# A product-key expert layer: v rows gathered expert-major and summed by 32-column matmuls

## The chip, the cores and the metric

The kernel runs on one core of a Trainium2 chip. The metric is the device time of one launch in microseconds, median of three runs.

## The reference, cut to what matters

One step of a transformer trunk over 512 prompt frames and 64 sample frames, width 1024, float32. Per layer: an input projection, two kinds of attention (8 heads of width 64, 4 heads of width 128), an output projection, LayerNorm, and then a PEER layer (product-key retrieval of single-neuron experts) and a second LayerNorm. The PEER layer is where the change lies. Each frame picks 16 experts in each of 8 heads, so 128 of 16,384; every expert is one row of `u_tab` and one of `v_tab`, 1024 floats (4 KB) each:

```python
q = (xs @ w_pq).reshape(PEER_BLOCK, PEER_HEADS, 2, PEER_QDIM // 2)
sc = jnp.einsum('thpd,hpnd->thpn', q, sub_keys)      # scores of 2 x 128 keys a head
s, i = lax.top_k(sc, PEER_TOPK)
...                                                   # top 16 of the 16 x 16 sums: eidx, g
hid = jnp.einsum('td,thkd->thk', xs, u_tab[eidx])
a = (g * gelu(hid)).astype(xs.dtype)
return jnp.einsum('thk,thkd->td', a, v_tab[eidx])
```

## The kernel before, in words

The frames are worked in five blocks: 0 to 3 are 128 prompt frames each, block 4 (`SMP`) is the 64 sample frames, laid twice on the 128 partitions. A block's PEER work is 128 *slots*; in slot k every partition (frame) deals with its own k-th expert. Block 4 has 64 slots, each half of the partitions taking half of a frame's experts. That makes 576 slots (`JSLOTS`).

A slot costs one gather of 128 u rows and one of 128 v rows (POOL, `gather`, L1670; an indirect DMA of 128 x 4 KB, its row numbers one column of `idx`). VectorE multiplies the u rows with x1 and sums along the row (L1598), which gives one column of `hid`. ScalarE applies Gelu to four columns at once (L1200) and multiplies each by the gate weight g, giving `coef` (L1208). Then the v rows are weighted and added in one of two ways, chosen by `on_tensor(k)`: on PE for 464 of the 576 slots, with a 128x128 diagonal of the coefficients that ScalarE makes (L1229) as stationary operand and two 512-column halves into the accumulator `acc` (L959, `j_tensor`); the profile shows two passes per float32 matmul, so four records a slot. On VectorE for the other 112, which multiplies by `coef` and adds into `y_acc` (L1610). `y_acc` starts as ALPHA * x1 on ScalarE (L1221); `f_vector` adds `acc` to it and takes the statistics; `n_vector` and `n_tensor` apply the LayerNorm; `y_store` writes it out.

All engines' instruction lists are written by one planner, `weave`: each lane (x projection, a attention, o output, w query, t top-k, j slots, f and n final norm) has a start and an end on a common axis of slot steps (`spans`), and each engine issues the lanes' steps in the order of their marks. An engine works in order, so one waiting instruction holds all behind it. In lane j, VectorE takes u row k at step k+3 and v row k is used at step k+11 (`V_LAG`). POOL issues u row j and then v row j-8 (`V_AT`), one after the other. Block p+1's attention and projections run among block p's slots.

Buffers: six u rows (`URING`) and six v rows (`VRING`) of 4 KB per partition, to which spare tiles are added late (`U_MORE`, `V_MORE`). A gather waits until the row before it in its buffer has been used. Weights stream on SP's queue through `wring`, five tiles of 512 KB; four of the eight w_v tiles (`HELD`) stay resident in `held`. Block 1's first 14 projection tiles are loaded early into buffers that lie idle then.

## Time and profile before

| | |
|---|---|
| runs | 1899.32 us median (1895.7 to 1900.65, three runs) |
| profiled execution, first to last instruction | 1895.5 us; its time with what lies around it isn't shown apart, the runs' median is 3.8 us above |
| mean granted PE clock | 0.964 |
| PE busy | 1601.3 us (84%), 6192 matmuls |
| VectorE (DVE) busy | 1263.2 us (67%) |
| ScalarE (ACT) busy | 627.4 us (33%) |
| GpSimd (POOL) busy | 1245.3 us (66%) |
| DMA | 744.60 MB, mean 393 GB/s; indirect gathers 605.75 MB |

Busy shares are means over unlike stages. A matmul's end is modelled, and consecutive ones overlap, so PE's busy time is not PE at its peak. A releaser behind an arrow is what ended an engine's idle time. In the windows the engines stand in the order PE, PE weight load, DVE, ACT, POOL, and of a filtered window only the engine asked for stands there.

### The profile page before, as it was taken

To read this page: it belongs to the slowest core of one execution; us is meant where nothing else is said; L and a number is where in the kernel's file an instruction comes from. 1 tells how busy PE (TensorE), PEld (TensorE's weight loads), DVE (VectorE), ACT (ScalarE), POOL (GpSimd) and SP (SyncE) were. 2 spreads that over 40 slices of the span, in tenths; PEclk is the share of its full clock that TensorE was granted. 3 is DMA by queue.
4 is the path that set the end of the run, shared out by engine and by line. 5 is a ranking of instruction groups with operands and counts; after the bars stand their busy time and mean duration, and the time that the engine had idled before them with its cause. 6 is when DMAs were issued, how large, how long until landed. Compare 5 with 4: busy or idle time off the path is not lost.

```text
span 1895.5 us, 20537 instructions
## 1 busy us (share of the span) xinstructions
PE 1601.3 (84%) x6192; PEld 881.4 (47%) x6192; DVE 1263.2 (67%) x2836; ACT 627.4 (33%) x1771; POOL 1245.3 (66%) x1199
## 2 busy tenths in 40 slices
PE   8999779879978698888898889998689877767877
PEld 7596445536435355355354465634436422222322
DVE  2379984576767755868587647589756897655543
ACT  1432561223237422232276222136522232222211
POOL 3027676576677755777777665677777777777771
PEclk9999999999989999999999998998899999999999
DMA  9899999999999999999999999999999999999995
GB/s 318 309 347 371 410 393 387 410 409 409 386 412 409 409 401 409 406 408 409 411 406 393 397 406 377 406 409 370 405 411 409 409 410 409 409 409 409 410 409 225
DMA packets 210197, 744.60 MB, mean 393 GB/s; under 512 B 24640, under 2 KB 29544, under 8 KB 209960
## 3 DMA queue, kind: packets, MB, share of 16 engines
q0 software_dynamic: 166720, 605.75, 80.9%
q1 hardware_dynamic: 43368, 137.53, 19.0%
q8 instruction: 51, 0.84, 0.2%
q14 instruction: 58, 0.48, 0.1%
HBM read 736.03 MB, written 7.75 MB: 392 GB/s over the span
## 4 chain that ended last, share of the span: by engine, by line
DMA 35%; PE 30%; POOL 20%; issue 9%; DVE 6%; ACT 1%; SPq 0%; DVEq 0%; ACTq 0%
DMA vbuf<-in_peer_v,idx 18%; PE acc L959 10%; POOL ubuf L1670 9%; POOL vbuf L1670 8%; DMA ubuf<-in_peer_u,idx 8%; PE mixer L667 5%; DMA held<-in_peer_u,idx 4%; PE mixer L833 2%; PE mixer L936 2%; DVE ubuf L1598 2%; PE mixer L683 2%; DMA wring<-in_c_k 1%; POOL wring L1670 1%; DMA held<-in_peer_v,idx 1%; POOL held L1670 1%
## 5 line engine op out<-in xcount | busy, mean ns | idle before, releaser
L959 PE MATMUL acc<-vbuf,diag 128*128 128x512 f32 x1308 | 644.5, 627 | 159.5 <-DMA vbuf<-in_peer_v,idx 154.6
L1670 POOL DMA_INDIRECT ubuf<-in_peer_u,idx x518 | 553.9, 1069 | 255.5 <-issue 138.4
L1670 POOL DMA_INDIRECT vbuf<-in_peer_v,idx x478 | 512.4, 1072 | 264.4 <-PE acc L959 133.0
L1598 DVE CUSTOM_DVE_ANT_0 ubuf<-ubuf,x 128x1024 f32<-128x1024 f32 x332 | 404.9, 1224 | 252.9 <-DMA ubuf<-in_peer_u,idx 249.7
L959 PEld LDWEIGHTS acc<-vbuf,diag 128*128 128x128 f32 x1308 | 236.7, 196 | 470.4 <-issue 429.0
L1598 DVE CUSTOM_DVE_ANT_0 ubuf<-ubuf,mixer 128x1024 f32<-128x1024 f32 x186 | 225.6, 1218 | 118.2 <-DMA ubuf<-in_peer_u,idx 81.9
L1200 ACT ACTIVATE act_h<-hid 128x4 f32<-128x4 f32 x144 | 29.5, 205 | 504.1 <-DVE hid L1598 503.4
L936 PEld LDWEIGHTS mixer<-stage,wring 128*128 128x128 f32 x1280 | 149.5, 193 | 17.4 <-issue 15.4
L936 PE MATMUL mixer<-stage,wring 128*128 128x128 f32 x1280 | 150.6, 276 | 0.7 <-DMA wring<-in_w_pq 0.6
L1229 ACT ACTIVATE diag<-ident,coef 128x128 f32<-128x128 f32 x392 | 138.4, 395 | 22.1 <-PE acc L959 18.1
L1610 DVE SCALAR_TENSOR_TENSOR y_acc<-vbuf,coef,y_acc 128x1024 f32<-128x1024 f32 x99 | 127.3, 1286 | 18.1 <-DMA vbuf<-in_peer_v,idx 16.0
L667 PEld LDWEIGHTS mixer<-xT,wring 128*128 128x128 f32 x1056 | 123.4, 194 | 18.0 <-issue 18.0
L667 PE MATMUL mixer<-xT,wring 128*128 128x128 f32 (+1 forms) x1056 | 124.5, 277 | 5.7 <-DMA wring<-in_w_qk 5.7
L1208 ACT ACTIVATE coef<-act_h,g 128x1 f32<-128x1 f32 x576 | 122.8, 283 | 16.2
L1670 POOL DMA_INDIRECT held<-in_peer_v,idx x60 | 64.3, 1072 | 18.3 <-issue 15.9
L1164 ACT COPY stage<-mixer 128x256 f32<-128x256 f32 x40 | 14.9, 373 | 181.9 <-PE mixer L936 181.9
L959 PE MATMUL acc<-held,diag 128*128 128x512 f32 x92 | 47.7, 649 | 24.5 <-DMA held<-in_peer_v,idx 22.7
L1200 ACT ACT_TABLE_LOAD x52 | 66.7, 1283 | 0.9
L833 PE MATMUL mixer<-wring,stage 128*128 128x512 f32 x128 | 58.5, 602 | 1.7 <-DMA wring<-in_w_out 1.5
L1598 DVE CUSTOM_DVE_ANT_0 wring<-wring,mixer 128x1024 f32<-128x1024 f32 x30 | 36.6, 1222 | 30.8 <-DMA wring<-in_peer_u,idx 21.6
L720 PE MATMUL mixer<-kv,q_pad 128*128 128x128 f32 (+3 forms) x128 | 48.8, 464 | 6.3 <-DVE neg_max L1337 5.7
L959 PE MATMUL acc<-vbuf,xT 128*128 128x512 f32 x80 | 40.5, 631 | 14.1 <-DMA vbuf<-in_peer_v,idx 14.0
(266 smaller groups left out, 1959.1 us busy)
## 6 DMA issues: line engine op xcount, KB each, us to landing
wring<-in_w_pq SPq DMA_DIRECT2D x80, 512.0 KB, 8.1
wring<-in_w_qk SPq DMA_DIRECT2D x66, 512.0 KB, 7.6
wring<-in_w_out SPq DMA_DIRECT2D x40, 512.0 KB, 7.5
wring<-in_w_v SPq DMA_DIRECT2D x20, 512.0 KB, 7.5
ubuf<-in_peer_u,idx POOLq DMA_INDIRECT x518, 13.0
vbuf<-in_peer_v,idx POOLq DMA_INDIRECT x478, 12.7
wring<-in_c_k SPq DMA_DIRECT2D x8, 512.0 KB, 6.9
wring<-in_c_v SPq DMA_DIRECT2D x8, 512.0 KB, 7.9
```

Of the source, the lines that this page charges most:

```text
L667: last = pe.matmul(ps_o[:, q % 2, j * P:j * P + frames], w[:, c, :], xT[:, c, 0:frames], start=c == 0, stop=c == KT - 1)
L683: last = pe.matmul(ps_o[0:frames, hf, :], xT[:, k, 0:frames], w[:, c, :], start=k == 0, stop=k == KT - 1)
L720: last = pe.matmul(dst, q_pad[:, g_, half, :], kT[:, g_, 0:nk], start=True, stop=not fox)
L833: last = pe.matmul(sums[hf], mix[:, c, :], w[:, hf * 512:(hf + 1) * 512], start=c == 0, stop=c == KT - 1)
L936: last = pe.matmul(ps_o[:, t % 2, j * P:(j + 1) * P], w[:, c, :], mixT[:, c, :], start=c == 0, stop=c == KT - 1)
L959: last = pe.matmul(sums[hf], diags[D_PLAN[n][0]], v_buf[b][:, hf * 512:(hf + 1) * 512], start=first, stop=last_one)
L1200: nc.scalar.activation(act_h[:, c:c + GRP], hid[:, c:c + GRP], ACT.Gelu).then_inc(gelu_done, 1)
L1208: last = nc.scalar.activation(coef[:, c + i:c + i + 1], act_h[:, c + i:c + i + 1], ACT.Copy, scale=g[p % 2][:, at + i:at + i + 1])
L1229: nc.scalar.activation(diags[b], (ident2 if p == SMP else ident)[:, :], ACT.Copy, scale=coef[:, v % MARKS:v % MARKS + 1]).then_inc(diag_do ...
L1598: nc.vector.tensor_tensor_reduce(out=u, in0=u, in1=x, scale=1.0, scalar=0.0, op0=ALU.mult, op1=ALU.add, accum_out=hid[:, k % MARKS:k % MAR ...
L1610: nc.vector.scalar_tensor_tensor(y_acc[p % 2][:, :], v_buf[b], coef[:, v % MARKS:v % MARKS + 1], y_acc[p % 2][:, :], ALU.mult, ALU.add).th ...
L1670: pool.indirect_dma_start(buf, None, a[table], bass.IndirectOffsetOnAxis(ap=idx[p % 2][:, at:at + 1], axis=0)).then_inc(landed_, 16)
```

## The change

The v rows change sides. A *unit* is 32 slots. The unit's row numbers are transposed in 32x32 blocks on VectorE (`idx_v`), so one gather now brings, on the 32 partitions of each quarter, the 32 experts of one frame: four frames of 32 experts each instead of 128 frames of one (block 4: as many, with two frames of twice 32). The coefficients are transposed the same way and spread by VectorE into `mix_w`, a 128x32 stationary operand per row whose four (two) non-zero columns pick the frame. A v row is then summed by matmuls with 32 output columns, that is into 32 partitions of `acc`; which 32 goes round with k (`group_of`). PE takes two rows at a time (`QUAD = 2`), the halves outermost, so consecutive matmuls go to different groups. All 576 v rows go this way, none is added on VectorE, and no diagonal is made.

The frames stand in another order in `acc`, so ALPHA * x1 is placed in it by a permuted diagonal (`place`) as the block's first matmul; ScalarE copies `acc` out into `x1[p % 3]`, which replaces `y_acc`; and y is stored in 16 pieces of 8 frames (block 4: 4 of 16). Gelu runs once per unit of 32 columns. Because a unit's coefficients are there only when its 32 u rows are done, v row k is gathered beside u row k+32 (`V_AT` = 32, `V_LAG` = 35). The v ring has eight buffers instead of six, the u ring loses one late buffer, and `HELD` goes from 4 to 3.

```diff
-HELD = 4
+HELD = 3
-URING, VRING = 6, 6
-U_MORE, V_MORE = ((368, 1), (438, 2)), ((360, 3), (430, 3))
+URING, VRING = 6, 8
+U_MORE, V_MORE = ((438, 2),), ((360, 3), (430, 3))
+UNIT, QUAD = 32, 2
-U_LAG, H_LAG = 3, 2
-D_LAG = U_LAG + H_LAG + GRP - 1
-V_LAG = D_LAG + 3
+U_LAG = 3
+G_LAG, C_LAG = U_LAG + 1, U_LAG + 2
+V_LAG = UNIT + U_LAG
 V_AT = V_LAG - U_LAG
...
+def frame_of(k):
+    s = k % UNIT
+    return s % 2 * 16 + s // 2 if part_of(k) == SMP else s % 4 * 8 + s // 4
+def group_of(k):
+    return k % UNIT % (2 if part_of(k) == SMP else 4)
...
 def y_store(sp, p):
+            for j in range(runs):
+                for q in range(many):
+                    ...
+                    sp.dma_start(o["y"][to:to + rows, :], y[at:at + rows, :]).then_inc(out_y[p % 2], 16)
...
 def j_tensor(pe, _):
             for j in range(J_STEPS):
-                v = j - V_LAG
-                if v >= 0 and on_tensor(v):
+                v = j - V_LAG - QUAD + 1
+                if v >= 0 and v % QUAD == 0:
+                    if v == p * SLOTS:
+                        ...
+                        wait(pe, acc_read, 2 * p)
+                        for hf in range(2):
+                            ...
+                                pe.matmul(acc[:, c], place[:, :], x1[p % 3][:, c], start=True, stop=False)
+                    pe.wait_ge(w_made, v // 8 + 1)
+                    for k in range(v, v + QUAD):
+                        b, _, nth = V_PLAN[k]
+                        pe.wait_ge(v_in[b], 16 * (nth + 1))
                     for hf in range(2):
-                        last = pe.matmul(sums[hf], diags[D_PLAN[n][0]],
-                                         v_buf[b][:, hf * 512:(hf + 1) * 512], start=first, stop=last_one)
-                    last.then_inc(vP_used, 1)
+                        for k in range(v, v + QUAD):
+                            s, r = k % UNIT, 32 * group_of(k)
+                            last = pe.matmul(acc[r:r + 32, hf * 512:(hf + 1) * 512], mix_w[:, s * 32:(s + 1) * 32],
+                                             v_buf[V_PLAN[k][0]][:, hf * 512:(hf + 1) * 512], start=False,
+                                             stop=k >= end - (2 if p == SMP else 4))
+                            if hf:
+                                last.then_inc(vP_used, 1)
...
 def j_scalar(act, _):
+                k = j - G_LAG
+                if 0 <= k < JSLOTS and k % UNIT == UNIT - 1:
+                    act.wait_ge(u_used, k + 1)
+                    wait(act, coef_done, n - 1)
+                    nc.scalar.activation(act_h[:, h], hid[:, h], ACT.Gelu).then_inc(gelu_done, 1)
...
 def f_scalar(act, p):
+            act.wait_ge(vP_used, min((p + 1) * SLOTS, JSLOTS))
+            for hf in range(2):
+                nc.scalar.copy(y[0:frames, c], acc[0:frames, c]).then_inc(acc_read, 1)
...
 def decode(n, s):
+                    for w in pairs_ready(p, n):
+                        c = slice(w * UNIT, (w + 1) * UNIT)
+                        nc.vector.transpose(idx_v[p % 2][:, c], idx[p % 2][:, c]).then_inc(idxv_done, 1)
...
 def j_vector(dve, chain):
-                    nc.vector.scalar_tensor_tensor(y_acc[p % 2][:, :], v_buf[b], coef[:, v % MARKS:v % MARKS + 1],
-                                                   y_acc[p % 2][:, :], ALU.mult, ALU.add).then_inc(vD_used, 1)
+                k = j - C_LAG
+                if 0 <= k < JSLOTS and k % UNIT == UNIT - 1:
+                    dve.wait_ge(gelu_done, n + 1)
+                    link(nc.vector.tensor_tensor(coef[:, :], act_h[:, h], g[p % 2][:, at:at + UNIT], ALU.mult))
+                    nc.vector.transpose(coef_t[:, :], coef[:, :]).then_inc(coef_done, 1)
+                    dve.wait_ge(coef_done, n + 1)
+                if k >= UNIT - 1 and (k + 1) % 8 == 0:
+                    wait(dve, vP_used, (n - 1) * UNIT + 8 * (c + 1))
+                    ...
+                    nc.vector.tensor_tensor(diagonals(p, c), each, to, ALU.mult).then_inc(w_made, 1)
...
 def gather(pool, table, k):
+                if k % UNIT == 0:
+                    pool.wait_ge(idxv_done, k // UNIT + 1)
+                at += frame_of(k) - k % UNIT
+                rows = idx_v[p % 2][:, at:at + 1]
```

## Rows read from the trace of the kernel before

**Rows 1.** the page's 40 slices: DMA busy in tenths, and GB/s moved

```profile
DMA  9899999999999999999999999999999999999995
GB/s 318 309 347 371 410 393 387 410 409 409 386 412 409 409 401 409 406 408 409 411 406 393 397 406 377 406 409 370 405 411 409 409 410 409 409 409 409 410 409 225
```

**Rows 2.** windows: range, us, busy us (count) by engine, clock, DMA share, GB/s

```profile
0.00:110.00 110.00, 102.17 (x617) 76.56 (x618) 33.47 (x130) 30.01 (x90) 17.54 (x47) 1.00 0.91 313
110.00:205.00 95.00, 87.98 (x524) 65.64 (x523) 88.73 (x281) 30.64 (x78) 61.80 (x57) 0.98 0.98 374
205.00:350.00 145.00, 123.09 (x541) 75.47 (x541) 99.94 (x200) 64.70 (x179) 96.19 (x91) 0.99 1.01 397
350.00:1500.00 1150.00, 992.93 (x3924) 558.91 (x3923) 798.47 (x1740) 407.29 (x1092) 801.72 (x724) 0.96 1.02 403
1500.00:1870.00 370.00, 276.52 (x553) 97.14 (x552) 236.20 (x479) 91.53 (x326) 268.02 (x282) 0.97 1.03 410
```

**Rows 3.** the chain of waits, share of the span by engine

```profile
DMA 35%; PE 30%; POOL 20%; issue 9%; DVE 6%; ACT 1%; SPq 0%; DVEq 0%; ACTq 0%
```

**Rows 4.** groups of instructions: count, busy us, mean ns, idle before

```profile
L959 PE MATMUL acc<-vbuf,diag 128*128 128x512 f32 x1308 | 644.5, 627 | 159.5 <-DMA vbuf<-in_peer_v,idx 154.6 <-ACT diag L1229 4.6
L1610 DVE SCALAR_TENSOR_TENSOR y_acc<-vbuf,coef,y_acc 128x1024 f32<-128x1024 f32 x99 | 127.3, 1286 | 18.1 <-DMA vbuf<-in_peer_v,idx 16.0
L1229 ACT ACTIVATE diag<-ident,coef 128x128 f32<-128x128 f32 x392 | 138.4, 395 | 22.1 <-PE acc L959 18.1
L1208 ACT ACTIVATE coef<-act_h,g 128x1 f32<-128x1 f32 x576 | 122.8, 283 | 16.2
```

**Rows 5.** timeline of PE, one v row: start us, us, count, idle before

```profile
787.15 1.96 PE L959 MATMUL acc<-vbuf,diag 128*128 128x512 f32 x4 [0.60 <-DMA vbuf<-in_peer_v,idx]
```

**Rows 6.** timeline of VectorE: a product of 128x32 elements

```profile
132.10 0.19 DVE L1550 TENSOR_TENSOR best_v<-best_v,sum 128x32 f32<-128x32 f32 x1
```

**Rows 7.** windows of POOL's gathers alone: u rows, then v rows twice

```profile
112.00:204.60 92.60, 32.13 (x32) 0.98 0.98 375
...
112.00:204.60 92.60, 29.34 (x24) 0.98 0.98 375
...
350.00:1500.00 1150.00, 398.68 (x362) 0.96 1.02 403
```

**Rows 8.** windows of VectorE's v additions (L1610) alone

```profile
110.00:205.00 95.00, 10.24 (x8) 0.98 0.98 374
```

**Rows 9.** DMA issues: count, KB each, median us to landing

```profile
wring<-in_w_v SPq DMA_DIRECT2D x20, 512.0 KB, 7.5
```

**Rows 10.** windows of pieces under full rate

```profile
500.00:520.00 20.00, 20.00 (x48) 8.93 (x47) 14.53 (x29) 4.97 (x18) 14.33 (x14) 1.00 0.96 354
1170.00:1190.00 20.00, 20.00 (x113) 14.26 (x112) 13.66 (x48) 5.94 (x14) 10.48 (x10) 1.00 0.93 338
1300.00:1320.00 20.00, 18.27 (x75) 11.63 (x74) 19.79 (x29) 11.38 (x25) 12.62 (x10) 0.85 0.92 319
```

**Rows 11.** the end: POOL, DMA landing, PE, VectorE and SP

```profile
1850.13 0.93 POOL L1670 DMA_INDIRECT held<-in_peer_v,idx  x1 [0.30 <-issue]
1861.33 0.94 POOL L1670 DMA_INDIRECT wring<-in_peer_v,idx  x1 [1.63 <-PE mixer L959]
...
wring<-in_peer_v,idx POOLq DMA_INDIRECT x1, 17.9
...
1869.34 5.39 PE L959 MATMUL mixer<-held,xT 128*128 128x512 f32 x12 [0.61 <-DMA held<-in_peer_v,idx]
1874.56 5.31 PE L959 MATMUL mixer<-vbuf,xT 128*128 128x512 f32 x12
...
1885.06 1.29 DVE L1623 TENSOR_TENSOR y_acc<-y_acc,mixer 128x512 f32<-128x512 f32 x2 [15.89 <-PE mixer L959]
...
1892.01 0.48 SPq L622 DMA_DIRECT2D out_y<-y_acc  x1
```

**Rows 12.** windows of PE's v rows (L959) alone

```profile
350.00:1500.00 1150.00, 551.14 (x1117) 203.44 (x1116) 0.96 1.02 403
```

More of the change, by code:

```diff
@@ L59, in parts_of, with pairs_ready @@
     return ((0, 1), (1, 3), (3, 8)) if p == 0 else ((0, 4), (4, 8)) if p == SMP else ((0, 8),)
+def pairs_ready(p, n):
+    if p == SMP:
+        return range(PAIRS // 2) if n else ()
+    h0, h1 = parts_of(p)[n]
+    return range(h0 // 2, h1 // 2)
 def t_plan(p):
@@ L223, in spans @@
         end = float(min((p + 1) * SLOTS, JSLOTS) + V_LAG)
[L224 to L226 removed]
+        out.append(("f", p, 3, end + 1.0, end + 4.0))
+        rows = 433.0 if p == SMP - 2 else end + 5.0 if p > SMP - 2 else (p + 1) * SLOTS + 78.0
         out.append(("n", p, 2, rows, rows + (3.0 if p in (1, SMP) else 10.0)))
@@ L291, in build @@
         x1 = [sb(f"x1_{n}", [P, D]) for n in range(3)]
-        y_acc = [sb(f"y_acc{n}", [P, D]) for n in range(2)]
         stage = sb("stage", [P, 5 * SEQ])
@@ L352, in build @@
         idx = [sb(f"idx{n}", [P, SLOTS], U32) for n in range(2)]
+        idx_v = [sb(f"idx_v{n}", [P, SLOTS], U32) for n in range(2)]
         g = [sb(f"g{n}", [P, SLOTS]) for n in range(2)]
@@ L1612, in j_vector @@
                 yield
         def f_vector(dve, p, chain):
-            link, y, n = chain.link, y_acc[p % 2], p % 2
-            end = min((p + 1) * SLOTS, JSLOTS)
-            dve.wait_ge(vP_used, PE_COUNT[end])
-            wait(dve, vD_used, end - PE_COUNT[end])
-            if p == SMP:
-                dve.wait_ge(acc_made, NB)
-            if p == SMP:
-                for hf in range(2):
-                    last = nc.vector.tensor_tensor(y[:, hf * 512:(hf + 1) * 512], y[:, hf * 512:(hf + 1) * 512], acc_s[hf], ALU.add)
-            else:
-                last = nc.vector.tensor_tensor(y[:, :], y[:, :], acc[:, :], ALU.add)
@@ L1626, in f_vector @@
-            last.then_inc(acc_read, 1)
-            dve.wait_ge(acc_read, p + 1)
+            link, y, n = chain.link, x1[p % 3], p % 2
+            yield
+            dve.wait_ge(acc_read, 2 * p + 2)
             for hf in range(2):
```

215 lines of the change are left out of this document (91 added, 124 removed).

## The prediction, made before the changed kernel ran

> **What bounds the kernel now.** I read the page first. The DMA line of its 40 slices is at 9 nearly throughout, and the line below it stands at about 409 GB/s from the fifth slice on [rows 1]. Then the windows by stage. From 1500 to 1870 us, where only table rows are gathered, 410 GB/s is held; no longer stretch is faster, so I take 410 GB/s as full rate. One gathered row tile (128 x 4 KB = 524,288 bytes) then costs 1.28 us of DMA, and a slot (one u, one v) 2.56 us. In the same windows PE is busy 75 to 93%, VectorE 64 to 93% [rows 2]. The chain of waits says the same less directly: DMA holds its largest share, PE the second [rows 3]. The groups and the timeline of PE show why PE is second: a v row costs it four passes, 1.96 us, and then it idles 0.60 us for the next one's DMA [rows 4, 5]. So PE follows DMA in the light stretches. The kernel is bound by bytes, except where the rate falls under 410. Valued as (1 - rate/410) x length [rows 2]: 26.0 us before 110 us (set-up, not touched), 8.3 us from 110 to 205, 4.6 us from 205 to 350, 19.6 us from 350 to 1500, none from 1500 to 1870. After that comes a drain. Work taken off an engine can therefore return at most what those losses and the drain hold, and whatever moves bytes out of a full stretch costs nothing, but out of a stretch into the end of the list costs its full price.
>
> **The change part by part.**
>
> *VectorE and ScalarE.* 112 of the 576 v rows are added on VectorE now, 144 us (110 of them show as two groups at 1.286 us, one of them [rows 4]). They go. In their place, per unit of 32 slots, stand six small operations (coefficient product, transpose, four weight fills of 128x32 elements). The trace has no such transpose; a 128x32 product took 0.19 us [rows 6], so about 1.2 us a unit, 22 us for 18 units; even at twice that VectorE gives back 100 us. ScalarE loses 464 diagonals at 0.395 us and 576 coefficients at 0.283 us [rows 4] (346 us) and gets 18 Gelus. Neither engine bounds in the mean, so this is worth only what it does inside the lossy stretches. Per unit VectorE now waits for one Gelu; behind it in its queue are the next u dot products, on which POOL's u gathers wait. The ring of six u buffers (6 x 1.28 us) covers a wait of a few us; I charge nothing, and without that cover it would be 18 waits.
>
> *PE.* 112 more rows go to PE, but each pair is written to two different 32-partition groups, the halves interleaved (row a, row b, row a, row b). If two column groups run beside each other, a pair costs about what a row costs now: one 1.96 us burst [rows 5]. 288 bursts instead of 464: PE gets lighter by some 340 us. Whether they do run beside each other no row of this trace shows: from below 1.96 us a pair, from above two serial rows, 3.9 us. I take the lower, because the operands, the number of passes and the bank are those of today's burst and only the output partitions differ; the upper is the first rival. The two extra start matmuls a block (place x x1) replace ScalarE's multiplication and go into the same accumulator: 5 x 1 us, hidden under PE's idle.
> The Trainium skill, "TensorE: Matmul & The Clock Gate", Part 3, speaks for and against: it reports three 32-column tiles at 2.38 times one, but also that a weight load overlaps matmuls in flight only when its row group differs, which column tiles of one contraction never do. By the first a pair is about 2 us, by the second it comes near the serial price. No row here decides.
>
> *The order of gathers.* Before, v row k is gathered beside u row k+8, now beside u row k+32. So in the first 32 steps u rows come alone and 32 v rows come alone at the end. Between 112 and 204.6 us, POOL issued 32 u rows and 24 v rows [rows 7]. Those 24 now come later: 24 x 1.28 = 30.7 us of DMA time put behind a bandwidth-bound remainder. What is won against it: in this stretch VectorE is busy 88.7 of 95 us (top-k of block 0, u dots), 10.2 of which are v additions [rows 2, 8]. VectorE, not DMA, then sets the pace, so step 32 is reached about 11 us earlier (between 10.2 and, if all idle time went too, 16.5). PE was full there as well, but it drops its v rows and is not late. Net +19.7 us (14 to 20.5).
>
> *Bytes.* HELD goes from 4 to 3, so one more w_v tile is streamed in blocks 1 to 4: 4 x 1.28 = +5.1 us. The w_v group shows today's four tiles in each of five blocks [rows 9]. The y stores carry the same bytes in 16 small DMAs a block; SP has idle time for them except at the end.
>
> *Losses that shrink.* 4.6 + 19.6 = 24.2 us are lost between 205 and 1500 us. The worst pieces: 338 GB/s at 1170 us with PE full, 354 at 500 us with PE full and VectorE decoding, 319 at 1300 us with VectorE at 19.8 of 20 us [rows 10]. PE at half the price per row and eight v buffers instead of six cure the first kind; the top-k and memset bursts of VectorE remain, the u ring stays at six, and one late u buffer is dropped. I take half: -12 us (0 to -24).
>
> *The end.* Now: the last v gather is issued at 1861.33 and lands 17.9 us later, at 1879.2; PE, which has been nine rows behind since 1869.34, is waited for until 1885.06; the end is 1895.5 [rows 11]. After: PE is level with DMA, because the coefficients of the last 32 slots are ready long before their rows. POOL issues a gather in 0.93 + 0.30 = 1.23 us [rows 11], still under 1.28, so v rows alone keep the full rate. Behind the last landing: one burst 1.96, then the same 10.5 us of norm and store, with the 1.29 us addition replaced by two ScalarE copies of about the same length, and three more store issues of 0.48 us [rows 11]: 1.96 + 10.5 + 1.4 = 13.9 against 16.3 us today: -2.4 us (-0.5 with the upper price of a pair).
>
> *Sum* on the profiled execution's span: 1895.5 + 19.7 + 5.1 - 12 - 2.4 = 1905.9 us. The median of the runs is 3.8 us above that span (1899.32); the same offset gives 1909.7 us, +0.5%. The likeliest case's own range is 1899 to 1921.
>
> **Rivals.**
>
> *1. The pairs do not overlap on PE.* Then every row costs at least the back-to-back price, (1874.56 - 1869.34)/3 = 1.74 us [rows 11], and there are 112 more of them. From 350 to 1500 us PE does 1117/4 = 279 of 362 v rows [rows 7, 12] and idles 1150 - 993 = 157 us; 83 more rows want 144 us of it. For: PE is already full in the pieces of rows 10. Against: much of its idle time is spread evenly and can be used. If a quarter of it shows as delay, +36; nothing is recovered, +12; and 32 v rows alone at the end pace by PE, 32 x (1.74 - 1.28) = +15. 1909.7 + 63 = about 1973 us. It decides once a pair costs over 2.56 us in the v-only end; from 350 to 1500 us PE's other work takes 993 - 551 = 442 us [rows 2, 12], so 181 pairs fill the rest at (1150 - 442)/181 = 3.9 us each, and bite earlier where that work is dense. (By the skill's rule on weight loads, told above, it would come out this way.)
>
> *2. The losses go entirely and the start costs less.* Step 32 at 16.5 us less, all 24.2 us recovered: 1895.5 + 14.2 + 5.1 - 24.2 - 2.4 + 3.8 = 1892 us, 0.4% faster. For: VectorE loses a tenth of its work in every lossy piece. Against: the 1300 us and 500 us pieces are VectorE's own bursts. It needs both, since either alone stays above 1893.6.
>
> *3. The unit's chain is exposed.* VectorE waits in order for ScalarE's Gelu, and PE for VectorE's weights. If 1.5 us a unit shows: 18 x 1.5 = 27, about 1937 us. For: ScalarE takes the Gelu behind its attention work in program order. Against: rings of six u and eight v rows hold some 18 us of DMA work.
>
> **How the numbers follow.** Forecast 0.52, rival 1 0.23, rival 2 0.20, rival 3 0.05. A difference under 0.3% (5.7 us: 1893.6 to 1905.0) can't be told from none. The lower part of the forecast's own range, about 0.2, and a little of rival 2 fall there: same 0.22. Faster, nearly all rival 2: 0.19. Slower: 0.59. The range must take in rival 2 in part and most of rival 1, which ends anywhere from 1950 up: 1889 to 1965.
>
> **What would show it.** Right: bytes up by 2.1 MB; from 112 us to the 32nd u gather about 81 us instead of 92.6, at under 310 GB/s; v groups on PE with bursts of eight passes (two rows) of about 2 us and PE busy some 300 us less; 410 GB/s until the last landing, with v rows alone for some 41 us, and about 14 us behind it. Wrong: bursts of eight passes that last 3.5 us (rival 1, with PE full and the rate under 400 in dense stretches); 408 GB/s or more from 205 to 1500 (rival 2); VectorE idle before its coefficient product, behind ScalarE (rival 3); a first stretch that keeps its 374 GB/s would break the largest term.

## The result: 26 us slower, and the profile after

| | before | after |
|---|---|---|
| median of the runs, us | 1898.32 (1895.7 to 1900.65, 4 runs) | 1924.28 (1922.49 to 1927.75, 4 runs) |
| ratio, 95% interval | | 1.0143 [1.0127, 1.016] |
| profiled execution, first to last instruction, us | 1895.5 | 1926.0 (its run: 1927.75) |
| mean granted PE clock | 0.964 | 0.871 |
| DMA | 744.60 MB, 393 GB/s | 746.65 MB, 388 GB/s |

The direction was forecast, the size was not: +10.4 us forecast, +26.0 us measured. Two later comparisons of the same two kernels gave 1.0152 [1.0115, 1.019] and 1.0134 [1.0109, 1.0159].

Eight of the experiments ran in two groups in which the kernel before itself took longer, group P (`a_held4_v7_u7`, `a_wring6_v7`, `b_held3`, `b_lag32`: 1987.6 us) and group Q (`b_lag32_b`, `b_wring6_v5`, `a_warm`, `a_wring6_warm`: 1983.0 us), so their total times are compared only within their group.

The page after: busy time by engine, PE by slices, the granted clock and the rate (the rate answers to [rows 1]).

```profile
PE 1438.7 (75%) x6660; PEld 692.9 (36%) x6660; DVE 1143.8 (59%) x2856; ACT 250.2 (13%) x546; POOL 1201.0 (62%) x1195
PE   8997789667787796677787869787698655555756
PEclk9999899888899898889899889898899777678789
GB/s 296 296 359 295 346 409 383 409 409 409 405 411 409 409 409 409 409 410 385 411 409 409 396 405 382 405 365 344 369 409 409 410 409 409 410 409 410 409 410 249
```

Every engine has less to do (PE 163 us, VectorE 119, ScalarE 377, POOL 44), and the kernel is slower. The rate shows two places: the first five slices, and slices 27 to 29 (about 1250 to 1400 us). The windows by stage after, columns as in [rows 2]:

```profile
0.00:110.00 110.00, 100.42 (x579) 73.44 (x580) 30.16 (x119) 29.25 (x88) 16.57 (x43) 0.98 0.89 305
110.00:205.00 95.00, 80.24 (x548) 67.97 (x547) 90.03 (x309) 18.93 (x44) 37.36 (x40) 0.91 0.89 325
205.00:350.00 145.00, 117.76 (x601) 64.10 (x600) 84.22 (x200) 26.53 (x68) 92.89 (x89) 0.93 0.99 385
350.00:1500.00 1150.00, 888.91 (x4209) 435.37 (x4209) 700.58 (x1710) 161.03 (x324) 759.52 (x717) 0.88 1.01 400
1500.00:1870.00 370.00, 213.98 (x586) 42.89 (x586) 231.45 (x505) 11.60 (x17) 273.95 (x286) 0.75 1.03 410
```

Valued as the prediction did, (1 - rate/410) x length, the time lost in the five stages is 28.2, 19.7, 8.8, 28.0 and 0 us after, against 26.0, 8.3, 4.6, 19.6 and 0 before. Between 205 and 1500 us, where I had expected 12 us back, 12.6 us more are lost.

To place the difference I compared POOL's issue of the same gather in both traces (u row k after less u row k before; k counts the gathers in order, 576 of each kind in both traces). The last gathers after, and behind them the end, which answer to [rows 11]; columns: start us, us, engine, line:

```profile
1852.46 0.94 POOL L1681 DMA_INDIRECT wring<-in_peer_u,idx  x1 [0.37 <-DVE hid L1602]
...
1899.19 0.94 POOL L1681 DMA_INDIRECT vbuf<-in_peer_v,idx_v  x1 [0.30 <-issue]
...
1913.46 1.91 PE L980 MATMUL acc<-vbuf,mix_w 128*32 128x512 f32 x8 [0.58 <-DMA vbuf<-in_peer_v,idx_v]
...
1915.42 1.06 ACT L1227 COPY x<-acc 64x512 f32<-64x512 f32 x2 [42.50 <-PE acc L980]
...
1921.42 0.69 DVE L1650 TENSOR_TENSOR x<-x,mixer 128x512 f32<-128x512 f32 x1
```

| stretch | forecast, us | measured in the trace, us |
|---|---|---|
| set-up, to u row 0 | 0 | +4.2 |
| u rows 0 to 32 | -11 | -13.0 (79.6 us for 32 instead of 92.6) |
| u rows 32 to 352 | } | -4.9 |
| u rows 352 to 400 (block 4's attention) | } +5.1 - 12 | +20.4 |
| u rows 400 to 575 | } | -0.6 |
| v rows after the last u row | +30.7 | +31.8 |
| last v row's issue to its landing (17.9 to 14.3 us) | 0 | -3.6 |
| its landing to the end (16.3 to 12.5 us) | -2.4 | -3.8 |
| sum | +10.4 | +30.5 |

The sum is the spans' difference. This profiled run was the slowest of the four, 3.5 us above their median, which accounts for most of the step from 30.5 to 26.0. The three bracketed rows together were forecast at -6.9 (5.1 for the bytes less 12) and came to +14.9. Nearly the whole miss is in one stretch of 48 gathers.

**What happens in that stretch.** PE from 1318 us after, columns as above:

```profile
1318.80 3.75 PE L789 MATMUL mixer<-wring,q_pad 128*128 128x512 f32 x4 [3.87 <-DMA wring<-in_c_k]
...
1322.80 2.98 PE L980 MATMUL acc<-vbuf,mix_w 128*32 128x512 f32 x8
1325.71 0.66 PE L804 MATMUL mixer<-ident,kv 128*128 128x128 f32 x4
1326.20 1.95 PE L820 MATMUL mixer<-wring,kv 128*128 128x128 f32 x16
...
1328.49 1.91 PE L980 MATMUL acc<-vbuf,mix_w 128*32 128x512 f32 x8
1330.34 0.74 PE L804 MATMUL mixer<-ident,kv 128*64 128x128 f32 x5
1336.11 3.75 PE L789 MATMUL mixer<-wring,q_pad 128*128 128x512 f32 x4 [5.04 <-DMA wring<-in_c_k]
```

L789 makes the scores from the cached keys, L804 transposes them, L820 multiplies with the cached values, and L980 is a pair of v rows. One group of block 4's attention takes 17.3 us here (1318.80 to 1336.11). PE is through with its work at 1331, then waits 5.04 us for the tile of cached keys, and the scores that follow (L789) run at 3.75 us for four passes, the lower of the two clock levels. VectorE stands behind the same scores, with the next u products behind it in its queue, and POOL behind those. VectorE, its first instruction after the scores, and the waits between 1300 and 1350 us:

```profile
1323.05 1.29 DVE L1377 CUSTOM_DVE_ANT_0 kv<-mixer,kv 128x1088 f32<-128x1088 f32 x1 [8.80 <-PE mixer L789]
```

```profile
DVE kv L1377 <- PE mixer L789: 23.8, 3, 11.0
...
POOL ubuf L1681 <- DVE hid L1602: 15.7, 4, 6.7
PE mixer L789 <- DMA wring<-in_c_k: 12.1, 3, 5.0
```

So the chain is: key tile late, scores late and slow, VectorE idle up to 11.0 us, no u buffer free for up to 6.7 us, transfers stop. The windows of these 160 us after, in quarters:

```profile
1240.00:1280.00 40.00, 33.74 (x116) 11.86 (x117) 29.08 (x72) 6.36 (x12) 23.76 (x24) 0.87 1.01 391
1280.00:1320.00 40.00, 28.83 (x125) 13.28 (x124) 29.80 (x46) 7.83 (x18) 29.05 (x24) 0.89 0.97 358
1320.00:1360.00 40.00, 29.59 (x111) 13.29 (x110) 15.14 (x30) 10.38 (x18) 18.56 (x18) 0.77 0.90 333
1360.00:1400.00 40.00, 26.49 (x128) 11.31 (x128) 22.23 (x42) 6.55 (x15) 31.80 (x26) 0.83 0.96 374
```

No engine is full: VectorE is busy 15.14 of 40 us where the rate is 333 GB/s. Before, the windows of the same four read 409, 364, 403 and 411 GB/s.

**Why a turn of this loop is longer.** SP's own waits from 1290 to 1360 us after:

```profile
SPq L553 <- PE mixer L820: 59.0, 4, 16.4
```

SP asks for the next key tile when PE has done with a value tile (L820; L806 before). The same turn before the change (L775 scores, L790 transposes, L806 values, L959 a v row):

```profile
1325.37 2.54 PE L775 MATMUL mixer<-wring,q_pad 128*128 128x512 f32 x4 [3.16 <-DMA wring<-in_c_k]
...
1328.87 2.50 PE L806 MATMUL mixer<-wring,kv 128*128 128x128 f32 x16
...
1331.71 1.98 PE L959 MATMUL acc<-vbuf,diag 128*128 128x512 f32 x4
...
1333.64 1.88 PE L959 MATMUL acc<-vbuf,diag 128*128 128x512 f32 x4
...
1338.87 2.39 PE L775 MATMUL mixer<-wring,q_pad 128*128 128x512 f32 x4 [2.91 <-DMA wring<-in_c_k]
```

In each kernel four turns have such a wait. From the request for the tile to the start of the scores they took 6.1, 7.3, 7.1 and 6.9 us before and 6.0, 6.4, 7.5 and 7.8 after, which is nearly the same. From the start of the scores to the next request they took 4.8, 6.4, 6.4 and 4.8 us before and 8.4, 9.8, 9.7 and 9.4 after, 14.9 us more in all. Two things fill that part. Before, both v rows of a turn stood behind the product with the values, where PE would have waited for the tile anyway; after, one pair (2.06 to 2.98 us, 10.5 in all) stands between the scores and that product and so delays the request. And the scores take 3.29 to 3.75 us for 1.95 to 2.54, 5.7 more in all. The other pieces are 1.4 us shorter. With the 0.3 us from request to scores this makes 15.2 of the 20.4 us. It is read from two traces; no run moved the pair behind the product.

### The profile page after: what moved, and what is told of

Same layout as the page of the kernel before. It is cut to its first block, busy times and chain, and to the rows that moved or that the text cites. A ratio compares the mean times of both kernels' runs of the same rounds, so it can differ in the third digit from the quotient of the medians.

```text
span 1926.0 us, 19624 instructions
## 1 busy us (share of the span) xinstructions
PE 1438.7 (75%) x6660; PEld 692.9 (36%) x6660; DVE 1143.8 (59%) x2856; ACT 250.2 (13%) x546; POOL 1201.0 (62%) x1195
## 2 busy tenths in 40 slices
DMA packets 211261, 746.65 MB, mean 388 GB/s; under 512 B 25201, under 2 KB 30105, under 8 KB 211033
## 4 chain that ended last, share of the span: by engine, by line
DMA 45%; POOL 19%; PE 18%; issue 9%; DVE 7%; SPq 0%; ACT 0%; POOLq 0%; DVEq 0%; ACTq 0%
DMA ubuf<-in_peer_u,idx 22%; DMA vbuf<-in_peer_v,idx_v 18%; POOL ubuf L1681 9%; POOL vbuf L1681 8%; PE acc L980 6%; PE mixer L681 3%; DVE ubuf L1602 2%; PE mixer L847 2%; POOL wring L1681 2%; PE mixer L950 2%; DMA wring<-in_c_k 1%; PE mixer L789 1%; POOL held L1681 1%; DMA wring<-in_w_qk 1%; DMA wring<-in_peer_u,idx 1%
## 5 line engine op out<-in xcount | busy, mean ns | idle before, releaser
L980 PE MATMUL acc<-vbuf,mix_w 128*32 128x512 f32 x1968 | 629.2, 737 | 328.6 <-DMA vbuf<-in_peer_v,idx_v 244.8
L1681 POOL DMA_INDIRECT vbuf<-in_peer_v,idx_v x492 | 511.9, 1040 | 169.5 <-issue 132.1
L980 PEld LDWEIGHTS acc<-vbuf,mix_w 128*32 128x32 f32 x1968 | 123.1, 124 | 664.0 <-issue 540.2
L980 PE MATMUL acc<-held,mix_w 128*32 128x512 f32 x204 | 88.4, 758 | 51.6 <-DMA vbuf<-in_peer_v,idx_v 23.4
L980 PE MATMUL acc<-wring,mix_w 128*32 128x512 f32 x132 | 54.0, 776 | 38.8 <-DMA wring<-in_peer_v,idx_v 15.3
L1681 POOL DMA_INDIRECT held<-in_peer_v,idx_v x51 | 53.2, 1043 | 19.8 <-issue 12.8
L980 PEld LDWEIGHTS acc<-held,mix_w 128*32 128x32 f32 x204 | 15.9, 124 | 109.3 <-issue 91.6
L761 PE MATMUL mixer<-kv,stage 128*128 128x64 f32 (+1 forms) x320 | 46.9, 279 | 1.8 <-ACT x L1067 1.4
L1334 DVE CUSTOM_DVE_ANT_0 stage<-mixer,bias 128x128 f32<-128x128 f32 (+3 forms) x64 | 31.2, 487 | 28.4 <-PE mixer L736 17.2
L697 PE MATMUL mixer<-wring,xT 128*128 128x512 f32 (+1 forms) x100 | 47.5, 618 | 0.0
L1602 DVE DVE_READ_ACCUMULATOR2_ANT hid<- 128x1 f32 x576 | 47.3, 82 | 0.0
```

Of the source, the lines that this page charges most:

```text
L697: last = pe.matmul(ps_o[0:frames, hf, :], xT[:, k, 0:frames], w[:, c, :], start=k == 0, stop=k == KT - 1)
L761: last = pe.matmul(head_sums(p, m, width), pT2[m % 2][:, c, :], vS[:, c, col:col + width], start=c == 0, stop=c == nk // P - 1)
L980: last = pe.matmul(acc[r:r + 32, hf * 512:(hf + 1) * 512], mix_w[:, s * 32:(s + 1) * 32], v_buf[V_PLAN[k][0]][:, hf * 512:(hf + 1) * 512], ...
L1334: nc.vector.tensor_tensor_reduce(out=logit_p[m % 3][:, 0:nk], in0=ps_s[:, m % 2 * 512:m % 2 * 512 + nk], in1=bias_m, scale=-QSCALE, scalar ...
L1602: nc.vector.tensor_tensor_reduce(out=u, in0=u, in1=x, scale=1.0, scalar=0.0, op0=ALU.mult, op1=ALU.add, accum_out=hid[:, k % (2 * UNIT):k ...
L1681: pool.indirect_dma_start(buf, None, a[table], bass.IndirectOffsetOnAxis(ap=rows, axis=0)).then_inc(landed_, 16)
```

## The experiments

Theory 1: the miss lies in block 4's attention, where PE waits for tiles that pass through the ring `wring` one after the other. Theory 2: it lies in what the change gave up (`HELD`, one late u buffer). Theory 3: the order of the gathers costs more than the sum said. Theory 4: the pairs on PE are dearer than they look.

### More held tiles, or a longer tile ring

The SBUF is nearly full, so each tile is paid for with v buffers and tiles loaded early. `a_held4_v7_u7`:

```diff
-HELD = 3
+HELD = 4
-URING, VRING = 6, 8
-U_MORE, V_MORE = ((438, 2),), ((360, 3), (430, 3))
+URING, VRING = 6, 7
+U_MORE, V_MORE = ((368, 1), (438, 2)), ((360, 3), (430, 3))
-EARLY = 14
+EARLY = 13
```

> The changed kernel with HELD = 4 again (one w_v tile less to stream in blocks 1 to 4), the seventh u buffer back at slot 368, and seven v buffers instead of eight to pay for it (13 early tiles instead of 14). Theory A (the missing u buffer makes the stall around block 4's attention, where the changed kernel falls behind by 20 us between slots 352 and 400): set-up 4 us earlier, 5 us fewer bytes, and 15 or more of the 20 us back: about 1900 us. Theory B (that stage is a loop of PE, SP's tile ring and VectorE, whose length the u ring doesn't change): only 4 + 5 us, about 1915 us, and the 20 us stay. If v buffers were what counted it would be no faster than 1924 us.

Measured: ratio 1.0141 [1.0066, 1.0215]. That rules out its theory A (about 1.001); theory B (about 1.009) lies inside the interval, and so does no gain at all. The held tile and the late u buffer don't cure the stretch: PE's waits for the key tile sum to 17.8 us there (17.5 in the changed kernel). `a_wring6_v7`, run beside it:

```diff
-WRING = 5
+WRING = 6
-URING, VRING = 6, 8
+URING, VRING = 6, 7
-EARLY = 14
+EARLY = 13
```

> The changed kernel with six tiles in SP's weight ring instead of five, paid for with one v buffer (13 early tiles). In block 4's attention the key tile of a group is then requested one release earlier. Theory B (loop through the tile ring): PE's wait for in_c_k tiles there (17.5 us) goes, and 12 to 20 us of the 20 come back: about 1907 us. Theory A (u buffers): the stage keeps its 20 us, 1922 to 1926 us.

Measured: 1.0025 [0.9987, 1.0063], beside 1.0141 of the other. Run again with the changed kernel in the same group:

> Six weight tiles and seven v buffers in the changed kernel, once more beside the changed kernel itself: 15 to 20 us faster than it, because block 4's attention no longer waits for its key tiles (theory B). Under theory A the two are equal.

Measured: 1918.86 us, ratio 1.012 [1.0099, 1.0142]; the changed kernel beside it 1928.76 us. 5 to 10 us less, not the expected amount. The mechanism is nonetheless plain in its trace. The scores' passes (L789) of block 4, count and ns minimum/median/maximum, with what PE waited for before them and who waited for them; first the changed kernel:

```profile
L789 PE MATMUL mixer<-wring,q_pad x32: 592/1052/1222, 1248.0 to 1356.3; 128*128 128x512 f32 x32
...
  DMA wring<-in_c_k: 17.5, 4
...
  DVE kv L1377: 34.4, 4
```

and with six tiles:

```profile
L789 PE MATMUL mixer<-wring,q_pad x32: 592/593/1222, 1248.1 to 1338.9; 128*128 128x512 f32 x32
...
  DVE kv L1377: 0.9, 1
```

The wait for the tile is gone, the median pass falls from 1052 to 593 ns, VectorE's wait from 34.4 to 0.9 us. Gathers 352 to 400 take 2.1 us more than before instead of 20.4. The windows from 1280 to 1400 us, of the changed kernel and with six tiles:

```profile
1280.00:1400.00 120.00, 84.91 (x361) 37.88 (x361) 67.17 (x117) 24.76 (x50) 79.40 (x67) 0.83 0.94 355
```

```profile
1280.00:1400.00 120.00, 87.13 (x393) 39.17 (x392) 72.58 (x124) 25.68 (x52) 92.09 (x80) 0.87 1.01 395
```

Part was given back elsewhere. The time lost by the rate is 11.3 us less from 1280 to 1500 us (401 instead of 380 GB/s) and 1.6 and 2.1 us less in the first two stages, but 3.9 us more from 205 to 350 (374 instead of 385 GB/s) and 2.3 us more from 350 to 1280 (404 instead of 405): one v buffer and one early tile fewer. Net 8.8 us by this count, beside spans of 1926.0 and 1916.6.

`a_held4_wring6_v6` takes both (`WRING = 6`, `HELD = 4`, `VRING = 6`, `EARLY = 12`, late u buffer back):

> The changed kernel with HELD = 4, the u buffer at slot 368 and six weight tiles, paid for with two v buffers (six) and 12 early tiles. If the costs add (set-up 4, bytes 5, block 4's loop 15 to 20 us), it is 24 to 29 us faster than the changed kernel, about the time of the kernel before; what then stays of the change is the delayed v rows against the lighter VectorE and PE. If eight v buffers matter, it gives part of that back.

Measured: 1921.14 us, ratio 1.0126 [1.0109, 1.0143], 7.6 us under the changed kernel beside it and not 24 to 29. The gains don't add. The set-up's +4.2 us is gone (+0.1) and the attention stretch is cured, but with six v buffers and two early tiles fewer u row 80 is issued 3.3 us earlier than before instead of 9.8: the start gives back what the tiles won. Buffers are worth different amounts at different times, and the SBUF has no room for all.

The changed kernel again, beside these:

> The changed kernel itself, as the measure for the others of this group on the same chip: 1.3 to 1.6% above the kernel before.

Measured: 1928.76 us, ratio 1.0152 [1.0115, 1.019]. In its trace gathers 352 to 400 cost 17.3 us; in a third one (below) 15.5. The stretch isn't stable from run to run. The other rows of the table are, within some 3 us, but for one: u rows 32 to 352 cost 3.9 us in `a_again` instead of -4.9, with the rate down to 181 GB/s from 1160 to 1180 us.

### The control: does the kernel before need a sixth tile?

```diff
-WRING = 5
+WRING = 6
-URING, VRING = 6, 6
+URING, VRING = 6, 5
-EARLY = 14
+EARLY = 13
```

> The kernel before with six streaming tiles instead of five (paid with one v buffer and one early tile). Control for the tile ring. Theory A (before, PE's v rows were paced by their own DMA, and the tile of in_c_k was hidden behind them, so a sixth tile matters only after the change): between -3 and +6 us. Theory B (the ring of five is a bottleneck of both kernels): 8 us or more under before.

Measured: 1.0049 [1.0015, 1.0083], about 10 us slower: as a whole it lost more than A allowed, and B's gain isn't there. But the whole doesn't answer for the stretch. PE's wait for the key tile there, in the kernel before and with six tiles:

```profile
PE mixer L775 <- DMA wring<-in_c_k: 10.5, 4, 3.2
```

```profile
PE mixer L775 <- DMA wring<-in_c_k: 1.1, 1, 1.1
```

u rows 352 to 400 take 153.0 us with six tiles, 156.6 in the kernel before, and 169.3 in `b_lag32_b` (below), the nearest to a kernel before in this group. So the sixth tile helps the stretch in the kernel before as well, though how much can't be said across groups. The loss is elsewhere: u rows 32 to 352 take 22.0 us more than in `b_lag32_b`, with one v buffer and one early tile fewer. The ring of five tiles was short before the change too; this control can't show that the change made it so.

### HELD alone

In the kernel before, `HELD = 3` and the late u buffer left out:

```diff
-HELD = 4
+HELD = 3
-U_MORE, V_MORE = ((368, 1), (438, 2)), ((360, 3), (430, 3))
+U_MORE, V_MORE = ((438, 2),), ((360, 3), (430, 3))
```

> The kernel before with HELD = 3 and without the u buffer added at slot 368, nothing else. Bytes +5 us and, if the later landing of the norm rows behind the extra streamed tile is what delays the changed kernel's set-up, +4 us: about 1908 us. Theory A adds 15 us or more in block 4's attention (1923 us or more), theory B little.

Measured: 1.0058 [1.0018, 1.0098], as expected from the bytes and the set-up; theory A's 15 us in block 4's attention are ruled out. Its first u gather is issued at 117.3 us; in `b_lag32`, of the same group and with four tiles held, at 113.5. That is +3.8, close to the changed kernel's +4.2. The tile that isn't held has to pass through the ring in block 0, ahead of the constants that PE waits for; in the changed kernel that wait reads

```profile
51.52 0.50 PE L734 MATMUL mixer<-kv,q_pad 128*128 128x128 f32 x2 [2.27 <-DMA d_neg<-in_ln]
```

This is the set-up cost that the prediction took as nothing. The held tile is not all of it: with the tile held again `a_held4_v7_u7` still issues its first u gather at 115.8 us, 2.3 later than `b_lag32` in its group, and six tiles without the held one (`a_wring6_v7_b`) bring it to 113.4, +1.3 over before.

### Two extra products against the low clock

Ahead of each wait for a key tile (7 groups), in `a_warm` on the changed kernel, in `a_wring6_warm` on the one with six tiles:

```diff
                     pe.wait_ge(max_done, MATS * p + g_)
+                    for _ in range(2):
+                        pe.matmul(ps_s[:, 0:512], ident[:, :], d_neg[:, 0:512], start=True, stop=True)
                 landed(pe, p, "ck", g_)
```

> The changed kernel with two extra 128x512 products into the free score banks ahead of each wait for a tile of in_c_k in block 4's attention (7 groups), so that PE does not stand idle there. Nothing else differs. Theory A (the tile's 7.5 us after its request set the pace, half clock only lengthens it): scores back from 3.75 to 2.0 - 2.7 us, 1 to 2 us less a group, 5 to 12 us under the changed kernel. Theory B (the latency alone sets the pace and there is slack behind the scores): within 3 us of it, with scores shorter. Theory C (PE is too full there): slower by 5 us or more.

Measured: 1.0167 [1.0134, 1.02]. One group of it:

```profile
1351.77 1.88 PE L786 MATMUL mixer<-d_neg,ident 128*128 128x512 f32 x4
1362.01 3.72 PE L791 MATMUL mixer<-wring,q_pad 128*128 128x512 f32 x4 [8.36 <-DMA wring<-in_c_k]
```

Where no wait came after the extra products the scores ran at 1.99 us, but here it was 8.36 us and the clock was low again; the median pass was 697 ns and the waits still 12.9 us. Theory A's gain isn't seen, though the changed kernel didn't run in this group (its ratio elsewhere is 1.0134 to 1.0152). The low clock comes with the wait and doesn't go without it. It isn't free either, since the slow scores are part of the turn above; how much of the 20 us it is, this run can't say.

> The changed kernel with six streaming tiles (seven v buffers, 13 early tiles) and the two extra products of a_warm. With six tiles PE did not wait for in_c_k and its scores ran at 593 ns a pass already, so there is nothing for the extra products to mend: Theory A: 0 to 6 us over the changed kernel with six tiles alone (which measured 1.012 of before), so 1.012 to 1.016. Theory B (the clock, not the wait, is what six tiles mended): faster than 1.010.

Measured: 1.0065 [1.004, 1.0089]; six tiles alone had 1.0025 and 1.012 in two other groups, so this doesn't separate A from B. Within its trace all four-pass scores have a median of 592 ns and no wait, as without the products: there was nothing to mend.

### The order within a pair

```diff
-                    for hf in range(2):
-                        for k in range(v, v + QUAD):
+                    for k in range(v, v + QUAD):
+                        for hf in range(2):
```

> The changed kernel with the two loops of a pair exchanged: both halves of row a, then both of row b, so that passes in a row go to the same 32-partition group and overlap only at the seam. A pair costs 3.2 us or more instead of 1.91 at full clock. If PE's time per row were what the change lives on, the time goes up by 15 us or more (the last 32 rows alone are paced by PE: (3.2 - 2.56) x 16 = +10). If PE is not the bound elsewhere, it is +10 to +15 and the granted clock rises from 0.87.

Measured: 1924.24 us, ratio 1.0141 [1.0124, 1.0158]: the same as the changed kernel (1.0152 beside it), and not 10 us or more above it, as expected. The pair still takes 1.92 us:

```profile
1009.77 1.92 PE L980 MATMUL acc<-vbuf,mix_w 128*32 128x512 f32 x8
```

Where the two rows of a pair lie in differently named buffers, their passes can be told apart: they start at 1901.57 (`held`), 1901.58 (`vbuf`), 1901.99 and 1902.03 us, side by side, though the program gives all four of one row first. The eight passes needn't alternate in the program for the two groups to run beside each other.

### No second group

All v rows but the last four of a block go to the same 32 partitions of `acc`; only the overlap is taken away, and the rows of all frames are added up in the first group's partitions:

```diff
-                            s, r = k % UNIT, 32 * group_of(k)
+                            s, r = k % UNIT, 32 * group_of(k) if k >= end - 4 else 0
```

> The changed kernel with all v rows but the last four of a block summed into the same 32 partitions of acc, so that consecutive passes never go to different groups (its sums are not the reference's; every gather, pass and wait is there). Theory A (the pair costs 1.91 us because two groups run beside each other, and this is what keeps v rows alone at full rate): a pair takes 3.5 to 3.9 us at full clock, PE busy up by over 400 us, the 32 v rows after the last u gather take 55 to 60 us instead of 47, and the time is that of rival 1 without its thrift, 20 to 60 us over the changed kernel. Theory B (32-column passes are short whatever group they go to): pairs stay near 1.9 us and the time within 3 us of the changed kernel.

Measured: 1973.87 us, ratio 1.0389 [1.0371, 1.0406], 49.6 us over the changed kernel. Theory A. The page's busy line, and a pair, a run of 26 passes and the last windows of it:

```profile
PE 1771.5 (89%) x6660; PEld 778.7 (39%) x6660; DVE 1139.0 (58%) x2856; ACT 250.8 (13%) x546; POOL 1205.2 (61%) x1195
```

```profile
789.41 3.59 PE L980 MATMUL acc<-vbuf,mix_w 128*32 128x512 f32 x8 [1.54 <-DMA vbuf<-in_peer_v,idx_v]
...
1943.95 11.32 PE L980 MATMUL acc<-vbuf,mix_w 128*32 128x512 f32 x26
```

```profile
1893.00:1949.00 56.00, 49.49 (x114) 12.24 (x115) 11.52 (x26) 0.23 (x1) 31.08 (x34) 1.00 0.98 369
```

A pair costs 3.59 us, back to back 8 x 11.32/26 = 3.48. The v rows after the last u gather take 55.5 us instead of 46.7, at 369 GB/s. This is the case of rival 1 of the prediction, worked out at 1973 us, and 49.6 us is what the overlap is worth. Its clock is 0.968: the changed kernel's 0.871 is the clock of an engine that has less to do.

This run also bears on block 4's attention. PE is back near its old price per v row, and the stretch is longer still: u rows 352 to 400 take 26.2 us more than before (20.4 in the changed kernel). PE waits only 10.2 us for the key tile, as before the change, VectorE 39.3 us for the scores, and each turn holds a pair of 3.62 us or more between the scores and the product with the values. So the loss doesn't need a PE that comes sooner to its waits.

### The order of the gathers alone

In the kernel before, v row k beside u row k+32, with 48 columns of `coef` instead of 16 to hold the coefficients so long:

```diff
-D_LAG = U_LAG + H_LAG + GRP - 1
+CMARKS = 48
+D_LAG = 32
-        coef = sb("coef", [P, MARKS])
+        coef = sb("coef", [P, CMARKS])
```

> The kernel before, with v row k gathered beside u row k+32 instead of k+8 and used at step k+35, all else as it was (diagonals, VectorE additions, six v buffers, HELD = 4). If the order of gathers costs what the prediction took for it, 24 rows of 1.28 us go from a stretch that VectorE paces to the end of the list, less the 10 us by which VectorE gets there sooner: +18 to +21 us, about 1918 us. The rival, that v rows moved out of a busy stretch cost nothing, gives 1899 us.

> The kernel before, with nothing but the order of gathers changed: v row k is gathered and used beside u row k+32 instead of k+8 (its coefficients are kept in 48 columns). Theory A (the order is worth what the prediction gave it, 24 x 1.28 = 30.7 us of v rows moved to the end against some 12 us won at the start): 16 to 22 us over the kernel before, ratio 1.009 to 1.012. Theory B (v additions and diagonals beside the u rows hide the late rows anyway, and the after kernel's loss lies in its unit structure): under 8 us, ratio under 1.004. In its trace, A wants v rows alone for 30 us more at the end and the 32nd u gather 7 to 13 us earlier.

Measured: 1.0147 [1.0062, 1.0232] in group P and 1.0152 [1.0123, 1.018] in group Q. A third time, with the changed kernel and a half step with `D_LAG = 20` in the same group:

> The kernel before with v row k beside u row k+32 instead of k+8, now beside the changed kernel itself and a half step (below) on one chip. Theory A (the order of the gathers costs what the prediction said, 30.7 us at the end against some 12 at the start, and accounts for most of the change's loss): 16 to 22 us over before, and below the changed kernel, whose other terms (bytes, set-up, block 4's attention against the shorter end) add 4 to 10 us. Theory B (order alone costs as much as the whole change, as two comparisons at 1.015 said where full rate at the end was lower): 26 us or more over before.

> The kernel before with v row k beside u row k+20: 12 rows moved to the end instead of 24. Theory A (end price in proportion, 12 x 1.28 = 15.4 us, and at the start the first 32 u rows share the time with 12 v rows instead of none, so some 6 us are won): 8 to 11 us over before. Theory B (VectorE sets the pace of the start as soon as a few v rows are gone, so the first 12 rows moved win nearly all that can be won): 3 to 5 us over before.

> The changed kernel again, as the mark for the two others on the same chip: 24 to 30 us over before (ratio 1.013 to 1.016).

Measured: 1940.85 us, 1.0234 [1.0207, 1.0261], for 32; 1915.91 us, 1.0095 [1.0066, 1.0125], for 20; 1926.36 us, 1.0134 [1.0109, 1.0159], for the changed kernel. The first is far above theory A and above the whole change, so it lies in theory B's range (26 us or more), though order alone turns out not to be all of it. The half step is above both of its theories. The end of `b_lag32_c` says why in part: PE in three lines, and its window.

```profile
1866.34 5.39 PE L960 MATMUL mixer<-held,diag 128*128 128x512 f32 x12 [0.60 <-DMA held<-in_peer_v,idx]
...
1892.16 7.03 PE L960 MATMUL mixer<-vbuf,diag 128*128 128x512 f32 x16
...
1919.63 3.60 PE L960 MATMUL mixer<-wring,diag 128*128 128x512 f32 x8
```

```profile
1880.00:1905.00 25.00, 25.00 (x59) 11.05 (x58) 0.00 (x0) 5.30 (x11) 13.11 (x14) 1.00 0.88 327
```

From 1866.34 to 1923.2 PE never stops: 33 rows at 1.72 us each, near the 1.74 of [rows 11], where the full rate would bring one every 1.28. The rate falls to 327 GB/s. The v rows after the last u gather take 58.5 us, 43.6 more than before; 30.7 of them are the 24 rows' transfer, the other 12.9 are PE. The changed kernel has the same rows to do in 46.7 us, since its pairs cost 0.96 us a row. So of the 38.2 us between the spans of `b_lag32_c` and before, 17.2 are the order as the prediction priced it (30.7 less the 13.5 won at the start) and 12.9 a PE that can't follow rows that come alone. Another 10.2 us are lost between u rows 32 and 575, 5.8 of them in block 4's attention (3.9 in `b_lag20`), 1.3 in the set-up, and 3.4 are won behind the last v gather.

At the start 24 rows moved win 13.5 us over the first 32 u gathers, and 12 rows moved 7.9 us. That is in proportion (theory A's assumption), and each row wins 0.6 us there and costs 1.28 us or more at the end.

## Why the prediction was right and wrong

**The bound: right but for one stretch.** Every engine was relieved, and in the windows at 409 GB/s and more the time followed the transfers. In block 4's attention neither an engine nor the DMA was full (333 GB/s); there a loop of waits set the pace.

**The order of gathers: right as priced.** +18.8 us measured (31.8 - 13.0) for +19.7. VectorE was indeed the pace of the start (90.03 of 95 us busy). In the kernel before the same order costs more, 38.2 us, for the reasons above; the price holds only because PE's pairs can follow the rows at the end.

**PE's pairs: right at full clock.** 1.91 us for a pair, and even 16 passes over four groups in 2.15 us. PE's busy time fell by 163 us only, not by 300 or more: its v rows went from 917.7 to 699.6 us, 2.43 us a pair in the mean, because many pairs run at the lower clock.

```profile
664.66 2.15 PE L980 MATMUL acc<-vbuf,mix_w 128*32 128x512 f32 x16
```

Of the two statements of the Trainium skill that the prediction weighed ("TensorE: Matmul & The Clock Gate", Part 3), the trace agrees with the one on column tiles: two and four groups run beside each other. The other, that a weight load overlaps passes in flight only when its row group differs, did not bring the serial price here; `a_one_group`, with the same loads, did (3.59 us).

**Bytes: right.** 2.05 MB more, 5.0 us at 410 GB/s, for 5.1.

**Set-up, "not touched": wrong by 4.2 us.** I counted the fourth w_v tile in blocks 1 to 4 only. In block 0 it is no extra transfer, but it left a place of its own for the shared ring, ahead of what PE waits for. `b_held3` shows +3.8 without the rest of the change; with the tile held and six tiles in the ring (`a_held4_wring6_v6`) it is +0.1, with the tile held but five tiles in the ring (`a_held4_v7_u7`) 2.3 remain.

**Losses that shrink, -12: the step that failed.** It said that PE at half the price and eight v buffers cure PE's full pieces, and that nothing new appears. The first half held in part: the piece at 500 us [rows 10] went from 354 to 400 GB/s, the one at 1170 us only moved to 1160 and reads 358. The second half failed. From 205 to 350 us the loss grew by 4.2 us, for which no run looked for a cause; from 350 to 1280 us it shrank by 2.3 us, which is 1 GB/s, the last digit of the windows; from 1280 to 1500 it grew by 10.7. I had read the 319 GB/s piece at 1300 us as VectorE's own burst, which it was (19.79 of 20 us), and didn't ask what paced the loop around it. What the runs showed in its place is the turn of key tile, scores, product with the values and next request, with rows 352 to 400 at +20.4 us. That a sixth tile removes the loss after the change (+2.1) is shown. That it brings nothing before the change is not: there too it took PE's wait away.

Why the turn got longer is read from the traces and not tested: 14.9 us more stand between the start of the scores and the next request, as a pair of v rows placed there and scores at the lower clock. A PE that comes sooner to its wait isn't needed for it, since with slow pairs (`a_one_group`) the stretch cost 26.2 us. How much of the loss is the order of the gathers (3.9 and 5.8 us in `b_lag20` and `b_lag32_c`) stays open. This was the case that rival 3 had in general form, an exposed wait, at another place: the unit's own chain cost nothing. VectorE waited 2.0 us for ScalarE's Gelu in all 18 units:

```profile
L1610 DVE TENSOR_TENSOR coef<-act_h,g 128x32 f32<-128x32 f32 x18 | 3.4, 190 | 2.0 <-ACT act_h L1219 2.0
```

The small operations themselves sum to 22.2 us (3.4, transposes 3.8, weight fills 13.7 and 1.3), as forecast.

**The end, -2.4: right but for 1.4 us.** As forecast, PE is no longer behind: before, nine rows waited for it [rows 11]; now it waits for the last pair. From the last landing (1913.46) to the end are 12.5 us instead of 13.9, mainly because the three more store issues show as 0.4 us (3.86 us from the first store's issue to the end, 3.49 before) and not as 1.4. The last row also landed 3.6 us sooner after its issue, which the sum had not; no run shows why.

**Rivals.** Rival 1's condition didn't hold. Put in by `a_one_group` it gave 1973.87 us, but that its price was 1973 is luck: it was to cost 63 us over a forecast of 1909.7 and cost 49.6 over 1924.28, and of the change against before 26.2 us lie in block 4's attention, which its sum doesn't have. Rival 2 needed the losses to go; they grew.

**What stays open.** With six tiles some 21 us remain over before, about what order (18.8) and bytes (5.1) ask for. Whether the pair moved behind the product with the values would give the stretch back with five tiles wasn't tried. Why the attention stretch costs between 15.5 and 20.4 us in three traces of the same kernel (and 12.1 in `a_rows_in_turn`, whose total is the same) I can't say. How much of the 13 us in `b_lag32_c` is only its six v buffers wasn't tried. No version ran below the kernel before; the best of the changed ones is six tiles, 1918.86 us.

## What to carry to other kernels

When tiles pass through a ring, look at the turn from a tile's arrival to the request that its release allows: work that stood behind the release, in the wait, is free there, and the same work put before it lengthens every turn. Here that part of the turn grew by 3.7 us, while the wait for the transfer stayed the same. And read a control by its stages: the run with six tiles in the kernel before was slower as a whole and still had the cure in the stretch that it was made for. In a kernel bound by bytes, price a reordering by what is put behind the last useful overlap: here each row moved from start to end won 0.6 us and cost 1.28. And ask whether the engine that consumes those rows can follow when they come alone, because the same rows cost 1.72 us each with one pass at a time and 0.96 us in pairs.

## What the runs showed of the hardware

- 32-column passes into different 32-partition groups of one accumulator run beside each other: 8 passes over two groups 1.91 us, 16 over four 2.15 us, 8 into one group 3.59 us. The order in the program may be row by row (1.92 us).
- PE with less to do was granted less clock: 0.871 at 75% busy, 0.968 at 89% with the same program otherwise. In the stage with table rows alone it fell to 0.75, at no cost: a pair then took up to 3.59 us, and 410 GB/s were held.

```profile
1601.38 3.59 PE L980 MATMUL acc<-vbuf,mix_w 128*32 128x512 f32 x8 [3.21 <-DMA vbuf<-in_peer_v,idx_v]
```

- After a wait of 3.87 or 5.04 us the next four passes of 512 columns took 3.75 us. With two products put ahead they took 1.99 where no wait followed, and 3.72 after a wait of 8.36 us.
